# The first transfers of a Strassen-like trunk in another order, without filler ahead of the first product, and its adding transfers in two groups

## The reference, cut to what matters

```
hn = rms_norm(x, norm1_g)
z = gelu(hn @ w_in)                      # 1024 x 4096
u, v = split(z)                          # 2048 each
v = layer_norm(v) * ln_g                 # by token
sv = einsum('gts,bnsge->bntge', tril(w_s), v_chunks) + b_s
x = x + (u * sv) @ w_out                 # 2048 -> 1024
x = x + square(relu(rms_norm(x, norm2_g) @ w1)) @ w2   # 1024 -> 4096 -> 1024
return rms_norm(x, final_g)
```

## Time and profile before

| | |
|---|---|
| profiled execution | 1067.01 us |
| its span | 1064.9 us |
| around the span | 2.1 us |
| PE busy | 1056.5 us, 99% |
| DVE, ACT, POOL busy | 798.8, 561.4, 44.5 us |
| chain that ended last | PE 98%, DMA 1% |
| mean granted clock | 0.998 |
| HBM traffic | 198 GB/s over the span |

### The profile page before, as it was taken

How to read it: one execution, slowest core, us unless ns; L and a number is a source line. 1 busy time by engine, 2 the same in 40 slices (tenths; PEclk the granted TensorE clock), 3 DMA queues, 4 the chain that set the end, 5 groups by cost and what they waited for, 6 DMA issues and landing times.

```text
span 1064.9 us, 13170 instructions
## 1 busy us (share of the span) xinstructions
PE 1056.5 (99%) x5040; PEld 928.1 (87%) x5040; DVE 798.8 (75%) x892; ACT 561.4 (53%) x883; POOL 44.5 (4%) x49
## 2 busy tenths in 40 slices
PE   9999999999999999999999999999999999999997
PEld 8888888889899888888888888888888888888886
DVE  6986666779789996899858457565599585777766
ACT  6864454553554444564874555455643443344456
POOL 0000100000000000111000000000000000000240
PEclk9999999999999999999999999999999999999999
DMA  9273369772876495755444636627878355343224
GB/s 323 73 166 151 112 208 307 180 262 98 320 281 229 156 338 201 200 190 160 151 166 158 198 118 213 208 106 278 323 296 317 135 218 198 119 158 119 82 77 159
DMA packets 89935, 206.40 MB, mean 194 GB/s; under 512 B 9560, under 2 KB 16240, under 8 KB 82672
## 3 DMA queue, kind: packets, MB, share of 16 engines
q1 hardware_dynamic: 86192, 195.32, 52.6%
q0 software_dynamic: 3488, 9.96, 3.9%
q10 hardware_dynamic: 192, 0.27, 0.1%
HBM read 143.67 MB, written 67.11 MB: 198 GB/s over the span
## 4 chain that ended last, share of the span: by engine, by line
PE 98%; DMA 1%; ACT 0%; DVE 0%; SPq 0%; issue 0%; ACTq 0%; DVEq 0%
PE banks L479 32%; PE banks L483 32%; PE banks L484 32%; PE banks L573 3%; DMA rows<-in_x_dram 1%; PE banks L618 0%; ACT rows L1195 0%; PE banks L604 0%; PE banks L529 0%; PE banks L534 0%; DVE rows L1706 0%; ACT spare L1228 0%; ACT rows L1477 0%; DVE ring_low L1536 0%; ACT ring_high L1047 0%
## 5 line engine op out<-in xcount | busy, mean ns | idle before, releaser
L1077 ACT ACTIVATE pair_high<-left_and_right 128x1024 fp32r<-128x1024 f32 x168 | 176.5, 1055 | 223.3 <-PE banks L479 183.9
L1536 DVE TENSOR_TENSOR ring_low<-left_and_right,ring_high 128x512 fp32r<-128x512 f32 x224 | 152.3, 690 | 160.9 <-ACT ring_high L1047 160.3
L1544 DVE TENSOR_TENSOR pair_low<-left_and_right,pair_high 128x1024 fp32r<-128x1024 f32 x168 | 205.1, 1235 | 84.2 <-ACT pair_high L1077 83.9
L479 PE MATMUL banks<-pair_high 128*128 128x512 f32 x672 | 254.9, 379 | 0.0
L483 PE MATMUL banks<-pair_low,pair_high 128*128 128x512 f32 x672 | 254.7, 379 | 0.0
L484 PE MATMUL banks<-pair_high,pair_low 128*128 128x512 f32 x672 | 254.7, 379 | 0.0
L1047 ACT ACTIVATE ring_high<-left_and_right 128x512 fp32r<-128x512 f32 x224 | 136.9, 626 | 206.6 <-PE banks L479 126.0
L479 PE MATMUL banks<-s_high,ring_high 128*128 128x512 f32 x384 | 145.8, 380 | 0.0
L483 PE MATMUL banks<-s_low,ring_high 128*128 128x512 f32 x384 | 145.5, 379 | 0.0
L484 PE MATMUL banks<-s_high,ring_low 128*128 128x512 f32 x384 | 145.5, 379 | 0.0
L484 PEld LDWEIGHTS banks<-pair_high,pair_low 128*128 128x128 f32 x672 | 127.0, 189 | 18.0
(11 more groups left out here) (147 smaller groups left out, 1244.6 us busy)
## 6 DMA issues: line engine op xcount, KB each, us to landing
left_and_right<-sums SPq DMA_DIRECT2D x40, 1024.0 KB, 7.5
sums<-rows SPq DMA_DIRECT2D x34, 1024.0 KB, 5.2
left_and_right<-in_mlp_w_dram SPq DMA_DIRECT2D x34, 1024.0 KB, 7.3
left_and_right<-in_a_w_in_dram SPq DMA_DIRECT2D x19, 1024.0 KB, 7.6
v_blocks<-rows SPq DMA_DIRECT2D x8, 1024.0 KB, 7.2
left_and_right<-in_a_w_out_dram SPq DMA_DIRECT2D x8, 1024.0 KB, 10.5
rows<-in_x_dram SPq DMA_DIRECT2D x7, 1024.0 KB, 8.8
right_sums<-in_mlp_w_dram POOLq DMA_DIRECT2D x6, 1024.0 KB, 11.2
```

Of the source, the lines that this page charges most:

```text
L479: first = nc.tensor.matmul(ps[:, bank, :], stat_high, mov_high, start=start, stop=False, skip_group_check=True)
L1077: nc.scalar.activation(pair_high[pair_entry(d, pos, k)][:, :, :], pair_of(d, pos, k), ACT.Copy)\
L1536: nc.vector.tensor_tensor(ring_low[k][:, :], right_place(n, pos)[:, k, :], ring_high[k][:, :].bitcast(F32), ALU.subtract).then_inc(low_don ...
L1544: nc.vector.tensor_tensor(pair_low[e][:, :, :], pair_of(d, pos, k), pair_high[e][:, :, :].bitcast(F32), ALU.subtract).then_inc(low_done, 1)
```

## The change

At the start, the second, third and fourth k-tile of the first rows come in one transfer (a11_rest, 384 columns) in place of two; the weights of b11 come as single k-tiles 1, 2 and 3, the first two of them behind these rows and ahead of a12; b21 comes in two halves, with a22 between them; ACT waits for the new semaphores at the tiles concerned. The last filler ahead of the first unit is dropped, and in the first unit the turn of k = 1 stands behind the four products with rows_low. ACT makes ring_high[1] ahead of a_high k = 1, DVE ring_low[1] ahead of a_low k = 1. POOL starts its first four transfers when b22 of n = 1 has landed, and waits for b22 of n = 2 only ahead of the fifth.

```diff
-        x_landed = {b: sem(f"x_landed_{b}") for b in ("a11_first", "a11_second", "a11_right", "a12", "a21", "a22")}
+        x_landed = {b: sem(f"x_landed_{b}") for b in ("a11_first", "a11_rest", "a12", "a21", "a22")}
+        third_landed = sem("third_landed")
+        b21_rest_landed = sem("b21_rest_landed")
@@ first_unit (PE)
-                first_turn(1)
                 pe.wait_ge(combo_low, 1)
                 for m in range(4):
                     c = slice(m * P, (m + 1) * P)
                     nc.tensor.matmul(ps[:, banks[m], :], rows_low[:, c], walked(ring_high[0][:, :]), start=False,
                                      stop=False, skip_group_check=True)
+                first_turn(1)
                 pe.wait_ge(low_done, unit(0, 0, 0) + 1)
@@ first_turn (PE)
-                pe.wait_ge(x_landed[["a11_first", "a11_second", "a11_right", "a11_right"][k]], 16)
+                pe.wait_ge(x_landed["a11_rest" if k else "a11_first"], 16)
@@ start of PE
             first_turn(0)
             turn_gains()
-            warm(2)
@@ start of SP
+            def load_k(b, first, end, signal):
+                i = places(0)[b]
+                sp.dma_start(quarter[i][:, first:end, :], weight(0, b)[:, first:end, :]).then_inc(signal, 16)
+
             load_x("a11_first", 0, 0, P)
-            sp.dma_start(quarter[0][:, 0:1, :], weight(0, "b11")[:, 0:1, :]).then_inc(first_landed, 16)
-            load_x("a11_second", 0, P, P)
-            sp.dma_start(quarter[0][:, 1:2, :], weight(0, "b11")[:, 1:2, :]).then_inc(second_landed, 16)
-            load_x("a11_right", 0, 2 * P, 2 * P)
+            load_k("b11", 0, 1, first_landed)
+            load_x("a11_rest", 0, P, 3 * P)
+            load_k("b11", 1, 2, second_landed)
+            load_k("b11", 2, 3, third_landed)
             load_x("a12", 0, NB, NB)
-            load(("b11", 0), quarter[0][:, 2:4, :], weight(0, "b11")[:, 2:4, :], quarter_landed[0], "quarter0")
+            load(("b11", 0), quarter[0][:, 3:4, :], weight(0, "b11")[:, 3:4, :], quarter_landed[0], "quarter0")
             load_x("a21", 4, 0, NB)
-            load_weight(0, "b21")
+            load(("b21", 0), quarter[1][:, 0:2, :], weight(0, "b21")[:, 0:2, :], quarter_landed[1], "quarter1")
             load_x("a22", 4, NB, NB)
+            load_k("b21", 2, 4, b21_rest_landed)
             load_weight(0, "b12")
@@ split_high (ACT)
                     act.wait_ge(second_landed, 16)
+                elif u == 2:
+                    act.wait_ge(third_landed, 16)
+                elif (n, pos) == (0, 1) and k >= 2:
+                    act.wait_ge(b21_rest_landed, 16)
@@ start of ACT
-            first_high(1)
             split_high(0, 0, 1)
+            first_high(1)
@@ start of DVE
-            first_low(1)
             split_low(0, 0, 1)
+            first_low(1)
@@ POOL
-            pool.wait_ge(*landed["b22", 2])
+            pool.wait_ge(*landed["b22", 1])
...
             pool.wait_ge(t_made["t1"], 32)
+            pool.wait_ge(*landed["b22", 2])
             nc.gpsimd.dma_start(t_of("t2"), t_of("t1")).then_inc(t_made["t2"], 16)
```

More of the change, by code:

```diff
@@ L1458, in _ @@
               .then_inc(drained[4], 1)
+            split_high(0, 0, 1)
             first_high(1)
-            split_high(0, 0, 1)
             first_high(2)
@@ L2183, in _ @@
             nc.vector.tensor_copy(gains[:, KT:], ps[:, 6, 0:JT]).then_inc(drained[6], 1)
+            split_low(0, 0, 1)
             first_low(1)
-            split_low(0, 0, 1)
             first_low(2)
```

## The result

The changed kernel takes 1067.62 us (median of 21 runs, 1066.64 to 1068.74), the kernel before 1066.31 (21 runs, 1065.43 to 1067.34). The ratio is 1.0012 with a 95% interval of 1.0007 to 1.0018: 1.3 us slower, at least 0.7 and at most 1.9. The forecast was 1066.5, a gain of 0.3. The difference stays within the 0.2% that I had called "the same", but the direction was wrong.

The account below looks back on a forecast made before the run. TensorE (PE), working 99% of the span, was taken as the bound. Start +0.5 and adding transfers -0.8 gave -0.3 us: 1066.7 on the profiled execution, 1066.5 for the median, range 1065.2 to 1068.0.

Parts of the forecast that it names:

- the place near 227: PE's one wait in the body, 0.8 us for a ring_low slice from DVE, expected to go.
- part 1: Order of the first transfers and the start: +0.75 - 0.23 = +0.5 us, between -0.7 and +1.65.
- weights k1 land at 9.15: At the start, weights of k = 1 land 0.3 before 9.45; first unit then begins at 11.4, against 10.66.
- the loss at 15: A product slot at 15.02 is 0.45 long, not 0.22; gain 0.23 us, bounds 0 and 0.23.
- at no cost: Four rows_low products (0.87 us) run ahead of turn k1, in PE's wait between 7.4 and 8.5, adding nothing.
- part 2: POOL's adding transfers in two groups: spare lands 3.1 us earlier, PE's wait goes; gain 0.8 us, bounds 0 and 0.82.
- the 2.1 us around the span: Time outside the profiled span, taken as unchanged: span 1064.6 to 1066.7 on the profiled execution.
- Rival B: Weights of k = 1 land late, ring_high heading ACT's order holds back a_high; 1067.4 to 1068.2, chance 0.25.
- Rival A: Early landings at the start: delay belonged to small packets, weights k1 land near 8.0; 1065.3, chance 0.2.
- Rival C: The clock: less filler brings PE's low level, half of 3.9 us lost; 1068.5, chance 0.05.
- Rival D: Reload of b21 at 121.62 slower beside four transfers, PE loses 0.1 to 1 us; about 1067, chance 0.05.
- Second half of b21: Behind a22 it lands at 21.2, ACT's third slice 1.1 us later; cost 0, up to 0.5 if PE is early.

Follow-up runs that it names:

- g2: Changed kernel with the rows of k = 1 and of k = 2, 3 apart again, weights of k = 1 between them; 1066.66 us, 1.0004 against before.
- e1: Changed kernel with the filler (two products of zeros) put back ahead of the first unit; 1067.13 us, 1.0010 against before.
- e4: Changed kernel with POOL's adding transfers in one group as before, so the start alone; 1067.07 us, 1.0009 against before.
- e3: Kernel before with only POOL's adding transfers in two groups; 1066.08 us, 1.0000 against before.
- f1: Changed kernel with the weights of k = 1 issued ahead of the merged rows; 1067.27 us, 1.0009 against before.
- c2: Kernel before with POOL's last adding transfer held back by a wait for a later DVE ring slice, issued at 208.75; 1068.62 us, 1.0019 against before.
- e2: Kernel before with only the last filler ahead of the first unit taken out; 1066.03 us, 0.9997 against before.
- g1: Kernel before with only the rows of k = 1 to 3 merged in one transfer, ahead of the weights of k = 1; 1067.15 us, 1.0006 against before.
- c1: Kernel before with POOL's last adding transfer held back by a mark that came too early, issued at 204.03; 1066.06 us, 0.9996 against before.
- n1: Kernel before, unchanged, run again for a second trace; 1066.10 us, 0.9998 against before.
- f2: Changed kernel with ACT's and DVE's order for k = 1 put back (a_high ahead of ring_high, a_low ahead of ring_low); 1067.83 us, 1.0012 against before.
- b1: Kernel before with adding transfers in two groups and the four rows_low products ahead of the turn of k = 1; 1066.69 us, 1.0002 against before.

## Why the prediction was wrong, point by point

**The bound.** Right: PE's products are the chain in every trace, and within the span only the start and the place near 227 moved (in g2 also 24).

**The first step that failed: part 1, "weights k1 land at 9.15", and with it the +0.5.** It is right in kind, too small in size. They landed at 9.51 in the first trace and at 9.58 and 10.15 in e1 and e4. The first unit in the traces of the six kernels with the merge begins at 12.24 on average (11.87 to 12.51), against 11.4 forecast, and by the spans of its 21 runs the changed kernel's begins at 12.50 on average. The trace, with 11.87, was one of its fastest. e3, with the start of before, has 11.08 for the start and the loss at 15 together. So part 1 is +1.4 where I had +0.5. I took the 0.3 for small packets from the line between two packet times; nothing of it came back. I also made the weights the cause. f1 shows that the rows, landing whole at 8.7 to 9.9, end as late by themselves: PE's 2.4 us behind the rows and the 2.36 behind the weights are two paths of nearly one length. And "at no cost" for the four products with rows_low took the full clock for granted: in the trace of the changed kernel they ran at the low level, and the turn behind them began at 9.13, though its rows had landed at 8.7. There the weights' path hid it.

**The second: part 2, "0.8 is all that PE can win", a gain of 0.8.** The mechanism was right in each link (last adding transfer beside spare's load, ACT, DVE, PE), and c2 shows it. Wrong was to book a loss seen in one execution as a loss of all. It was 1.15 in that one, 0.5 in the second trace of the same kernel, and 0 in e2, e4 and g1, which had the same one group: a mean of 0.33 over five traces. The spans give 11.32 - 11.08 = 0.24, which is within the noise. What makes the loss come and go stays open. The three traces without it have a late first unit (12.1 to 12.5) and spare's load issued at 210.2 to 210.6, those with it an early one (10.66, 10.65) and 209.0; no run separates this from chance. An early start doesn't bring it by itself: c1 has one (10.65) and lost nothing, and the fastest of the 33 runs has a span of 1063.2, which leaves 10.3 for the start and every loss.

**The third, and smallest: the 2.1 us around the span**, which I carried over. They are 2.24 with the second group.

**The sum as measured:** +1.4 - 0.2 + 0.14 = +1.3, where I had +0.5 - 0.8 + 0 = -0.3.

**Rival B** was the right one (measured 1067.62, its 1067.4 to 1068.2), with its place in part: the merged rows, not only ACT's order. **Rival A** fell: no landing was early. **Rival C**: I said that the only low stretch stood at the end. It stands at the start too, in what the products take, and the trace of before had it: four turns took 1.06 us at 3.91 and 0.66 at 7.40. The chain of n1, four turns of the same kind early and later:
```profile
4.12 0.85 PE banks L604 x4
...
7.41 0.44 PE banks L604 x4
```
Before's timeline of PE:
```profile
3.91 1.06 PE L604 MATMUL banks<-ident,rows 128*128 128x128 f32 x4
...
7.40 0.66 PE L604 MATMUL banks<-ident,rows 128*128 128x128 f32 x4
```
But this last piece of filler doesn't decide when it ends, and taking it out alone cost nothing measurable. **Rival D** did not come: PE waited nowhere between 121 and 160.

**The loss at 15** went, 0.25 for 0.23. **Second half of b21**: no cost here, and 0.8 where PE is early (g2; 0.6 of it waiting), a little over the bound (0.5).

## What to carry to other kernels

Before a wait in one trace is booked as a gain, see whether it is there in a second trace, or ask what it depends on; a transfer off the path whose start drifts by 4 us makes a wait that comes and goes. The first rows that an engine needs want a small transfer of their own: whoever waits for a transfer waits for all of it (1.4 us in g1), and to merge it with what is needed 2 us later cost about 1 us here. A gap in which one engine idles may hold two chains of nearly equal length; undo each before naming one. And the spans of all runs say how far the traced one is from the usual: once a few traces show which stretches vary, the rest can be read from the spans.

## What the runs showed of the hardware that was not expected

- TensorE's change from 1.2 to 2.4 GHz at the start of a program, read from the spacing of the products, varies between executions of like kernels. The first four products took 1.1 to 1.25 us (before, e3, f2), 1.4 to 1.8 (n1, c1, e1, g2, g1) and 2.05 to 2.08 (c2, b1, after, e2, e4, f1). Each of the three sets has kernels with the last piece of filler and without it; the slow one has four of the six without and two of the eight with, which is too few to say that it does nothing. The granted clock reads 1.00 throughout.
- It costs 1.26 us in c2 (first unit at 11.91, 10.65 in n1) and 1.48 in e2 (12.13), where nothing hides it, and nothing in g1, where the merged rows are awaited anyway.
- One transfer of 768 KB in place of 256 and 512 KB: the first 128 columns land at 8.7 to 9.9 and not at 6.0 to 7.35.
- A load of 1 MB (spare) took 4.8 to 4.9 us with no adding transfer beside it, 5.0 to 5.3 where the last 2 us of one ran beside its start (e2, e4, g1), and 7.0 to 9.2 where 3.6 us or more of an adding transfer from HBM to HBM did (c1, n1, before, c2).
- One more wait in POOL's list goes with 0.14 us of device time outside the profiled span (nine kernels against five).
